# Modulation weights multiplied raw in 32-bit products over four column groups, token modulation on VectorE

## The reference

```
mod   = silu(c) @ w_ada + b_ada          # w_ada: 2048 x 12288
mod_c = silu(c_ctx) @ w_ada + b_ada
sh1, sc1, g1, sh2, sc2, g2 = split(mod, 6)
h  = rmsnorm(x,  norm1_g) * (1 + sc1)  + sh1
hc = rmsnorm(ctx, norm1_g) * (1 + csc1) + csh1
p  = h @ w_in                            # K, V, Q, Fourier, gates
kc, vc = hc @ w_in[:, K], hc @ w_in[:, V]
# attention, Fourier branch, gated merge, w_out
x = x + g1 * y
x = x + g2 * (relu(h2 @ w1) ** 2 @ w2)   # h2 = modulated rmsnorm(x)
out = rmsnorm(x, final_norm_g)
```

## Time and profile before

| what | value |
|---|---|
| median of 3 runs | 1613.29 us (1612.23 to 1614.71) |
| span of the profiled execution | 1612.2 us |
| nearest run to that span | 1612.23 us |
| PE busy / mean granted clock | 96% / 0.981 |
| DVE, ACT, POOL busy | 61%, 46%, 5% |
| DMA, mean over the span | 222 GB/s |

### The profile page before, as it was taken

How to read it: one execution, slowest core, us unless ns; L and a number is a source line. 1 busy time by engine, 2 the same in 40 slices (tenths; PEclk the granted TensorE clock), 3 DMA queues, 4 the chain that set the end, 5 groups by cost and what they waited for, 6 DMA issues and landing times.

```text
span 1612.2 us, 19582 instructions
## 1 busy us (share of the span) xinstructions
PE 1552.2 (96%) x7009; PEld 1261.1 (78%) x7009; DVE 989.5 (61%) x1066; ACT 740.0 (46%) x1008; POOL 75.6 (5%) x70
## 2 busy tenths in 40 slices
PE   4898999999999999999998999999999999999997
PEld 3676887787788877878776888888888888888885
DVE  4776855387766666887886744444454545555556
ACT  5776433264454445433444544443434444444443
POOL 0334200010000000000000000000000000000001
PEclk8899999999999999999999999999999999999998
DMA  9777857577566667978985666556665555555552
GB/s 341 254 267 285 293 192 272 176 245 255 174 222 214 213 222 259 335 245 298 344 292 192 185 184 185 183 170 189 185 196 191 181 193 190 193 194 194 192 194 85
DMA packets 108100, 357.62 MB, mean 222 GB/s; under 512 B 10888, under 2 KB 11912, under 8 KB 106888
## 3 DMA queue, kind: packets, MB, share of 16 engines
q1 hardware_dynamic: 105984, 351.32, 65.1%
q10 hardware_dynamic: 2056, 5.51, 0.9%
HBM read 354.68 MB, written 2.10 MB: 221 GB/s over the span
## 4 chain that ended last, share of the span: by engine, by line
PE 83%; DVE 3%; ACT 2%; issue 1%; DMA 1%; POOL 0%; DVEq 0%; POOLq 0%; SPq 0%; ACTq 0%
PE bank L1195 25%; PE bank L1197 25%; PE bank L1196 25%; PE bank L1333 2%; PE bank L1315 1%; PE bank L1432 1%; PE bank L1286 1%; ACT wh L588 1%; PE bank L1273 1%; DVE wl L901 1%; PE bank L1323 1%; DMA raw<-in_w_fourier 1%; DMA raw<-in_w_out 1%; DVE acc L921 1%; PE bank L1251 1%
## 5 line engine op out<-in xcount | busy, mean ns | idle before, releaser
L901 DVE TENSOR_TENSOR wl<-raw,wh 128x1024 fp32r<-128x1024 f32 x508 | 616.4, 1224 | 514.6 <-ACT wh L588 514.0
L588 ACT ACTIVATE wh<-raw 128x1024 fp32r<-128x1024 f32 x508 | 530.8, 1058 | 472.3 <-PE bank L1197 447.5
L1195 PE MATMUL bank<-wh,hT 128*128 128x512 f32 x512 | 210.3, 411 | 0.0
L1195 PE MATMUL bank<-wh,h2T 128*128 128x512 f32 x512 | 203.3, 397 | 2.1 <-DVE h2T L1082 2.1
L1197 PE MATMUL bank<-wh,hT 128*128 128x512 f32 x512 | 200.9, 392 | 0.0
L1197 PE MATMUL bank<-wh,h2T 128*128 128x512 f32 x512 | 200.4, 391 | 0.0
L1196 PE MATMUL bank<-wl,hT 128*128 128x512 f32 x512 | 200.3, 391 | 0.0
L1196 PE MATMUL bank<-wl,h2T 128*128 128x512 f32 x512 | 200.1, 391 | 0.0
L1195 PE MATMUL bank<-wh,hidS 128*128 128x512 f32 x512 | 199.3, 389 | 0.0
L1197 PE MATMUL bank<-wh,hidS 128*128 128x512 f32 x512 | 199.2, 389 | 0.0
L1196 PE MATMUL bank<-wl,hidS 128*128 128x512 f32 x512 | 199.2, 389 | 0.0
(11 more groups left out here) (174 smaller groups left out, 1718.2 us busy)
## 6 DMA issues: line engine op xcount, KB each, us to landing
raw<-in_w SPq DMA_DIRECT2D x256, 512.0 KB, 4.3
raw<-in_w_ada SPq DMA_DIRECT2D x192, 512.0 KB, 5.1
raw<-in_w_in SPq DMA_DIRECT2D x128, 512.0 KB, 4.4
raw<-in_w_attn_o SPq DMA_DIRECT2D x32, 512.0 KB, 6.4
raw<-in_w_out SPq DMA_DIRECT2D x32, 512.0 KB, 6.6
raw<-in_w_fourier SPq DMA_DIRECT2D x16, 512.0 KB, 6.2
xt<-in_x ACTq DMA_DIRECT2D x2, 1024.0 KB, 9.5
ct<-in_ctx ACTq DMA_DIRECT2D x2, 1024.0 KB, 13.2
```

The source lines that it names most:

```text
L588: nc.scalar.activation(slot, raw[:, s % RAW, :], ACT.Copy).then_inc(wh_done, 1)
L901: nc.vector.tensor_tensor(lo, raw[:, s % RAW, :], hi.bitcast(F32), ALU.subtract)\
L1195: nc.tensor.matmul(bank[b][:], a_hi, w_hi, start=first, stop=False)
```

## The change

The 64 modulation tiles are no longer split. PE takes them as they land in `raw`, in true 32-bit products: 2 matmuls of 512 columns for a tile instead of 4, each with a stationary operand of 32 columns, `cc32`, in which two columns hold the SiLU vectors and thirty hold zeros. Row block kk writes PSUM partitions 32(kk mod 4) to 32(kk mod 4)+31, that is one of four column groups of the array; the two matmuls of a tile go to two different groups. `modrow` now has 128 rows, and `pair_sum` adds the four groups. SP may fill such a buffer again when PE is done with it (`gemm_done`). The tokens are modulated on DVE, ACT only rounds DVE's result, POOL has no part in it. Five instead of four K tiles stand among the modulation tiles, and side work follows two tiles behind instead of four. The counts of `wl_done` are renumbered (`NTH`, `W1`, `W2`), the spare split buffers are gone.

```diff
-MORE = 2
 AHEAD = 2
-AHEAD_MODS = 4
+AHEAD_MODS = 2
+GROUPS = 4
...
-K_AMONG = {("S1", 7), ("C1", 4), ("S2", 7), ("C2", 4)}
+K_AMONG = {("S1", 6), ("C1", 2), ("S2", 6), ("C2", 2), ("S3", 6)}
...
+SPLITS = [m for m, (name, _) in enumerate(TILES) if name not in MODS]
+NTH = {m: n for n, m in enumerate(SPLITS)}
+SLOT_OF = {m: n % SPL for m, n in NTH.items()}
+BEFORE = {m: SPLITS[n - SPL] if n >= SPL else None for m, n in NTH.items()}
+W1 = len(SPLITS)
+W2 = W1 + N1 * KT
...
-MODULATE = {K_AT[k] - 3: k for k in range(6)} | {K_AT[k]: k for k in (6, 7)}
+MODULATE = {K_AT[k] - 1: k for k in range(6)} | {K_AT[k]: k for k in (6, 7)}
...
-        cc4 = place("cc4", [P, 4 * KT + P], F32R, "acc", 1024)
+        pair_sum = place("pair_sum", [P, 2], F32, "acc", 512)
+
+        cc32 = place("cc32", [P, KT, P // GROUPS], F32, "acc", 1024)
...
-                if kind == "M":
-                    sp.wait_ge(wl_done, a + 1)
+                if kind == "M" and TILES[a][0] in MODS:
+                    sp.wait_ge(gemm_done, a + 1)
+                elif kind == "M":
+                    sp.wait_ge(wl_done, NTH[a] + 1)
...
-            for k in range(K_TILES):
-                for vv, src in enumerate((xhT, chT)):
-                    n = 2 * k + vv
-                    misc_wait_freed(pool, (("x", "c")[vv], k))
-                    pool.wait_ge(gain_ready, k // 2 + 1)
-                    if n >= 2:
-
-                        pool.wait_ge(h_lo, n - 1)
-                    for j in range(2):
-                        f = 2 * k + j
-                        nc.gpsimd.tensor_scalar(hmod[:, vv, j, :], src[:, f, :], gain1[:, f, vv:vv + 1],
-                                                mods[:, 0, f, vv:vv + 1], ALU.mult, ALU.add).then_inc(h_tmp, 1)
...
-                act.wait_ge(gain_ready, k // 2 + 1)
-                if k == 6:
-
-                    act.wait_ge(gemm_done, MORE_END)
-                for src, dst, vv in ((xhT, hT, 0), (chT, cT, 1)):
-                    misc_wait_freed(act, (("x", "c")[vv], k))
-                    for f in (2 * k, 2 * k + 1):
-                        nc.scalar.activation(dst[0][:, f, :], src[:, f, :], ACT.Identity,
-                                             bias=mods[:, 0, f, vv:vv + 1], scale=gain1[:, f, vv:vv + 1])\
-                            .then_inc(h_hi, 1)
+                for vv, dst in enumerate((hT, cT)):
+                    n = 2 * k + vv
+                    act.wait_ge(h_tmp, 2 * n + 2)
+                    nc.scalar.activation(dst[0][:, 2 * k:2 * k + 2, :], hmod[:, vv, :, :], ACT.Copy).then_inc(h_hi, 1)
...
-                split_hi(None if BEFORE[m] is None else BEFORE[m] + 1, s, hi_slot(m), 16 * (s // RAW + 1))
+                if name not in MODS:
+                    split_hi(None if BEFORE[m] is None else BEFORE[m] + 1, s, hi_slot(m), 16 * (s // RAW + 1))
...
+            dve.wait_ge(const_set, 3)
+            dve.wait_ge(cc_ready, 1)
+            nc.vector.tensor_copy(cc32[:, :, 0:2], cc[:]).then_inc(cc_ready, 1)
...
-            def modulate_lo(k):
+            def modulate(k):
+                dve.wait_ge(gain_ready, k // 2 + 1)
+                if k:
+
+                    dve.wait_ge(h_lo, 2 * k)
+                for vv, src in enumerate((xhT, chT)):
+                    misc_wait_freed(dve, (("x", "c")[vv], k))
+                    for j in range(2):
+                        f = 2 * k + j
+                        nc.vector.tensor_scalar(hmod[:, vv, j, :], src[:, f, :], gain1[:, f, vv:vv + 1],
+                                                mods[:, 0, f, vv:vv + 1], ALU.mult, ALU.add).then_inc(h_tmp, 1)
                 for vv, dst in enumerate((hT, cT)):
                     n = 2 * k + vv
                     dve.wait_ge(h_tmp, 2 * n + 2)
-                    dve.wait_ge(h_hi, 2 * n + 2)
+                    dve.wait_ge(h_hi, n + 1)
...
-                split_lo(m + 1, STREAM_AT["M", m], hi_slot(m), lo_slot(m))
+                if name not in MODS:
+                    split_lo(NTH[m] + 1, STREAM_AT["M", m], hi_slot(m), lo_slot(m))
                 if m in MOD_ADD:
                     mod_columns(MOD_ADD[m])
                 if m in MODULATE:
                     if MODULATE[m] == 6:
                         mod_columns(7)
-                    modulate_lo(MODULATE[m])
+                    modulate(MODULATE[m])
...
-                pe.wait_ge(wl_done, m + 1)
+                if name not in MODS:
+                    pe.wait_ge(wl_done, NTH[m] + 1)
                 if name in MODS:
 
                     p = MODS.index(name)
                     if p >= 2 and k == 0:
                         pe.wait_ge(modrow_ready, p - 1)
+                    s = STREAM_AT["M", m]
+                    pe.wait_ge(raw_full[s % RAW], 16 * (s // RAW + 1))
                     for j in range(2):
-                        for n_part, part in enumerate((hi_slot(m), lo_slot(m))):
-                            ins = nc.tensor.matmul(bank[MOD_BANK[name[0]]][:], cc4[:, 4 * (2 * k + j):4 * (2 * k + j) + P],
-                                                   part[:, j * HC:(j + 1) * HC],
-                                                   start=(k == 0 and j == 0 and n_part == 0),
-                                                   stop=(k == KT // 2 - 1 and j == 1 and n_part == 1))
+                        kk = 2 * k + j
+                        rows_k = slice(kk % GROUPS * P // GROUPS, (kk % GROUPS + 1) * P // GROUPS)
+                        ins = nc.tensor.matmul(bank[MOD_BANK[name[0]]][rows_k, :], cc32[:, kk, :],
+                                               raw[:, s % RAW, j * HC:(j + 1) * HC],
+                                               start=(kk < GROUPS), stop=(kk >= KT - GROUPS))
```

More of the change, by code:

```diff
@@ L78 @@
 CI1 = len(CHUNKS)
[L81 to L84, removed]
+SPLITS = [m for m, (name, _) in enumerate(TILES) if name not in MODS]
[4 more added lines that the diff above has]
+W2 = W1 + N1 * KT
+assert W1 % SPL == 0 and M1 % SPL == 0
 POSTS, _at = {}, 0
@@ L313, in hi_slot @@
         def hi_slot(m):
-            return wh[:, SLOT_OF[m], :] if SLOT_OF[m] < SPL else wh_more[SLOT_OF[m] - SPL][:]
+            return wh[:, SLOT_OF[m], :]
         def lo_slot(m):
-            return wl[:, SLOT_OF[m], :] if SLOT_OF[m] < SPL else wl_more[SLOT_OF[m] - SPL][:]
+            return wl[:, SLOT_OF[m], :]
         def wait_x2(eng, i):
@@ L505, in _ @@
             nc.gpsimd.memset(ones[:], 1.0).then_inc(const_set, 1)
-            nc.gpsimd.memset(cc4[:, 4 * KT:].bitcast(F32), 0.0).then_inc(const_set, 1)
+            nc.gpsimd.memset(cc32[:], 0.0).then_inc(const_set, 1)
             nc.gpsimd.memset(half_neg[:], -0.5).then_inc(const_set, 1)
@@ L563, in _ @@
             act.dma_start(ident[:], identity).then_inc(ident_in, 16)
-            for r in (0, 2):
-                act.dma_start(pair_sum[r:r + 2, :], identity[0:2, 0:2]).then_inc(ident_in, 16)
+            act.dma_start(pair_sum[:], pairs).then_inc(ident_in, 16)
             act.dma_start(rows[0:16, :], c.rearrange("(r n) -> r n", n=P)).then_inc(vec_in, 16)
@@ L578, in _ @@
                 .then_inc(tanh_ready, 1)
-            act.wait_ge(cc_ready, 1)
-            nc.scalar.activation(cc4[:, 0:4 * KT].rearrange("p (k v) -> p k v", v=4)[:, :, 0:2], cc[:], ACT.Copy)\
-                .then_inc(cc4_hi, 1)
             def split_hi(slot_wait, s, slot, n_raw):
@@ L645, in post @@
                         misc_wait_full(act, ("mod", p - 2))
-                    nc.scalar.activation(modrow[:, p % 2, :], bank[MOD_BANK[name[0]]][0:4, :], ACT.Copy)\
+                    nc.scalar.activation(modrow[:, p % 2, :], bank[MOD_BANK[name[0]]][:], ACT.Copy)\
                         .then_inc(modrow_ready, 1)
@@ L1212, in tile_products @@
                         ins.then_inc(bank_full, 1)
-            pe.wait_ge(ident_in, 48)
+            pe.wait_ge(ident_in, 32)
             pe.wait_ge(vec_in, 96)
@@ L1482, in _ @@
             for b in early:
-                pe.wait_ge(wl_done, M2 + N2 - 3 + b // 4)
+                pe.wait_ge(wl_done, W2 + N2 - 3 + b // 4)
                 last_products(b, [0], False)
@@ L1504, in constants @@
         "identity": np.eye(P, dtype=np.float32),
+        "pairs": np.tile(np.eye(P // GROUPS, 2, dtype=np.float32), (GROUPS, 1)),
         "dft": np.concatenate([cos, sin, -sin], axis=1).astype(np.float32),
```

29 lines of the change are left out of this document (10 added, 19 removed).

## The result

The changed kernel takes 1600.21 us in the median of 5 runs (1597.69 to 1604.14), the kernel before 1612.23 us in 5 runs beside it (1609.36 to 1614.71). The ratio is 0.9936, with a 95% interval of 0.9921 to 0.9951: 8 to 13 us faster, where 27.6 us were forecast. The direction held; the gain was 10 us by the ratio and 12 us by the medians. The profiled execution was the longest of the five, 1604.14 us with a span of 1602.4 us; the spans of the two profiled executions differ by 9.8 us.

A forecast was written before the change was run, and what follows sets the result against it. The first 150 us were held by the queue order of DMA, ACT, DVE and PE, the rest by PE. Modulation ending at 124 us plus 22.8 us ends K 27.6 us earlier: 1613.3 - 27.6, 1586 us; range 1570 to 1627.

The forecast's parts named there:

- PE's products: Modulation tiles on PE: two column groups work at a time, 0.86 us a tile, against 0.93 before.
- Rival 3: Modulation on PE: each record waits for its own weight load; 1638 to 1679 us; chance 0.05.
- DMA's sum: First stage: 40.4 MB at 340 GB/s plus 5 us end the last modulation tile at 124 us.
- at most seven buffers can fill: Ring while PE works on a K tile (5.5 us, cold more): some bandwidth is lost each time; 340 GB/s taken.
- Behind the last modulation tile: Until K ends: K tile 5 5.5, `pair_sum` 1.0, wait 3.6, cold clock 1.7, K tiles 6 and 7 11.0: 22.8 us.
- A shift of the first stage should arrive at the end unchanged: Stages from 175 to 1600 us: PE stays busy and untouched, so the gain of 27.6 us is carried through whole.
- Modulation on DVE: Token modulation: 0.3 us an operation (0.16 to 0.32), hidden by modulation tiles on PE except once, before K tile 6.
- The base: Starting time: profiled span 1612.2 us, as long as the fastest of three runs; difference taken from the median, 1613.3 us.
- Rival 2: First stage: groups overlap but the ring stays as empty, last modulation tile at 141 us; 1603 us; within the 0.74.
- Rival 1: Modulation on PE: column groups do not overlap, 1.72 us a tile, PE is the bound; 1625 us; chance 0.16.

The follow-up runs named there:

- K tile 4 behind: Changed kernel with K tile 4 moved back behind the modulation tiles, which also puts the `mac` tiles back: 1591.76 us, ratio 0.9874.
- warm clock: Changed kernel with three products that add zeros before the split waits of K tiles 0, 2 and 4: 1598.43 us, ratio 0.9917.

## Why the size was wrong, step by step

The mechanism held in the main: the groups overlap, PE no longer waits for the modulation tiles' splits, the DMA moves more, and K ends 15.1 us earlier. Three terms of the sum failed: the DMA's rate with K tiles in the way (7 us), K tile 5 without a wait or a cold clock (5.5 us), and later stages that change nothing (5.3 us).

*PE's products*: the assumption of two groups at a time was too low. Four run side by side: 32 records last 3.64 us in four groups, 7.06 in two and 13.92 in one. As the prediction said, this changes little; two groups cost 3.4 us only. The Trainium skill ("TensorE: Matmul & The Clock Gate", Part 3) says that products to different 32-partition groups run at the same time, and the traces agree. Its other sentence, that a weight load overlaps only when the row groups differ, is not borne out: all these products use the same rows, their loads take 0.109 us each, and the records came 0.098 us apart. Rival 3 fell with it:

```profile
L1347 PEld LDWEIGHTS bank<-raw,cc x256: 105/109/178, 10.6 to 130.0; 128*32 128x32 f32 x128
```

*DMA's sum* is the step that failed first. It took 340 GB/s for a stage with five K tiles in it and gave 124 us; it was 131. No K tile in the way gave 368 GB/s, so the DMA was sized well and the ring's stops at K tiles were not. With four K tiles in the way (K tile 4 behind) it was 39.8 MB until 123.7 us, 336 GB/s. The passage "at most seven buffers can fill" counted PE's 5.5 us for a K tile, a cold one more; it left out that the tile first passes ACT and DVE, up to 2.7 us in which PE waits. K tiles 0 and 4 took 7.2 and 8.4 us behind such waits, but K tile 2, behind one of 2.12 us, took 5.5. These waits are not the whole of it: with the loads three places ahead the last modulation tile ended 2.2 us earlier, with the warm clock 5.2 us (and 1.6 us earlier with the `mac` tiles in their old place, which changes nothing ahead of it, so single traces vary by as much). How the rest is shared between PE's own time for K tiles and the buffers they hold was not taken apart.

*Behind the last modulation tile*: the wait of 3.6 us before K tile 6 was right (3.72). But the same sum let K tile 5 run in 5.5 us without a wait. Its split has no cover, since a raw tile needs no split and PE is through with the tiles before it as soon as they land. 2.7 us of wait and 2.8 of cold clock are missing there. Before the change the last modulation tile had such a wait, 3.09 us, and K tile 4 behind it took 7.2: the row was in hand and was used for K tile 6 alone. The 1.7 us for the cold clock behind K tile 6's wait was the right kind of term: that tile took about 7.0 us.

*"A shift of the first stage should arrive at the end unchanged"* was wrong by 5.3 us. I looked at the busy share behind 175 us, and not at what the change does to lists that hang on `MODS_END`. With the `mac` tiles at their old place the stretch is even 3.3 us shorter than before. Which of DVE's operations between them and `g1row` makes out the difference was not taken apart.

*Modulation on DVE*: 0.41 us an operation, above even the 0.32 that was taken as the upper end, but in the chain it changed little. That the chain is hidden before K tiles 0 to 4 was right: the gaps there, which the prediction named as a sign that it is not, were waits for splits. With POOL those before K tiles 0 to 5 were longer by 2.9 us.

*The base*: the profiled execution before was not as long as the fastest of the three runs. In every run whose span is on record the time is 1.7 to 2.1 us above the span, so that execution took about 1614 us, near the longest. The forecast was taken from the median and does not move by this.

*Rival 2* (the DMA no better than now, 1603 us) had the nearest number, by luck and for another reason: the last modulation tile ended at 131 us and not at its 141, and more than half of the loss lay behind it. *Rival 1* was a true description of one group and mis-sized by 18 us. What stays open is 4 to 5 us between shifts in the spans and in the medians, for the early loading (7.3 and 3.2) and for the warm clock (7.2 and 1.8); 4.1 of them are the changed kernel's profiled execution, which was that much above its middle one.

## What to carry to other kernels

When one kind of tile loses a step of its pipeline, look at the tiles of the other kind that still have it: they arrive at the engine early, have no cover, and stop a shared ring. Load such tiles some places ahead of where they are used, and leave one of them between a result and what waits for it. And search for every table that is laid out from an index which the change moves (here `MODS_END`): it gave back a third of the shift, and a one-line edit undid it.

## What the runs showed of the hardware that was not expected

Four column groups of 32-bit products of 512 columns ran fully side by side: 32 records in 3.64 us, against 7.06 in two groups and 13.92 in one. Within one group of 32 columns a record took as long as one of 128 columns, 0.43 us. A group of four token transposes that stands between products of 32 columns takes 0.59 us (73.02 to 73.61) and not 0.36. Its neighbours differ in shape (32 columns for 128) and in type (32-bit for `float32r`), and which of the two costs the 0.23 us was not tested. And POOL's `hmod` fell from 1.75 to 0.80 us when DVE had less to do, with no change to POOL's own code: two operations took 7.11 us beside DVE's splits and 1.09 us with DVE idle.
